# MLP products of a hybrid diffusion trunk, in seven block products in place of eight for two of three token banks

## The reference

```python
mod = silu(cond) @ mod_w[l] + mod_b[l]            # sh1, sc1, g1, sh2, sc2, g2
h = rmsnorm(x, norm_mix[l]) * (1 + sc1) + sh1
x = x + g1 * mixer(h)                              # retention or recurrence
h = rmsnorm(x, norm_mlp[l]) * (1 + sc2) + sh2
x = x + g2 * (relu(h @ mlp_w1[l]) ** 2 @ mlp_w2[l])   # 1024 -> 4096 -> 1024
```

## Time and profile before

| | us |
|---|---|
| median of 3 runs | 2734.0 (2730.71 to 2734.75) |
| the profiled execution, time | 2731.88 |
| its span | 2730.1 |
| TensorE busy | 2609.2 (96%) |
| VectorE, ScalarE, GpSimd busy | 1641.1, 666.3, 699.7 |
| DMA, mean | 66 GB/s |

### The profile page before, as it was taken

The page is one execution under the profiler, slowest core; times in us unless marked ns, Lnnn a source line. Parts: engine busy times, 40 slices in busy tenths (PEclk is TensorE's granted clock), DMA queues, the critical chain, the costliest instruction groups (busy, mean ns, idle before and its releaser), DMA issues.

```text
span 2730.1 us, 39975 instructions
## 1 busy us (share of the span) xinstructions
PE 2609.2 (96%) x14730; PEld 2524.3 (92%) x14730; DVE 1641.1 (60%) x3056; ACT 666.3 (24%) x1016; POOL 699.7 (26%) x395
## 2 busy tenths in 40 slices
PE   7999999899999999999999889789999999999998
PEld 4999999899999999999998778678999999999997
DVE  5878778548567567567586777855433443442444
ACT  5323323232001001001044544423110110110113
POOL 0221212222222222222223323432222232222321
PEclk9999999999999999999999989899999999999998
DMA  6422222312222222222222101121111111111111
GB/s 235 146 70 69 82 67 71 124 47 66 63 81 69 64 82 69 61 85 69 62 73 104 38 21 36 59 77 31 47 39 42 43 38 46 38 44 41 38 46 70
DMA packets 259139, 181.18 MB, mean 66 GB/s; under 512 B 9205, under 2 KB 253685, under 8 KB 258166
## 3 DMA queue, kind: packets, MB, share of 16 engines
q1 hardware_dynamic: 257924, 169.99, 20.4%
q10 hardware_dynamic: 1138, 10.21, 1.0%
HBM read 165.48 MB, written 14.69 MB: 66 GB/s over the span
## 4 chain that ended last, share of the span: by engine, by line
PE 85%; DVE 9%; issue 3%; ACT 2%; DMA 0%; ACTq 0%; DVEq 0%; POOL 0%; POOLq 0%; SPq 0%
PE psum L588 80%; PE psum L862 2%; DVE mod_sum L1228 2%; DVE work_f L1624 1%; DVE h_lo L1254 1%; DVE sumsq L1197 1%; PE mod_psum L613 1%; DVE x L1275 1%; PE psum L668 1%; DVE sumsq L1260 1%; DVE h_hi L1598 1%; DVE mod_sum L1223 0%; DVE s_bwd L1474 0%; PE psum L743 0%; ACT rate_f L1107 0%
## 5 line engine op out<-in xcount | busy, mean ns | idle before, releaser
L588 PE MATMUL psum<-h_hi,w_hi 128*128 128x384 f32 (+1 forms) x2880 | 682.0, 345 | 36.4 <-DVE h_lo L1254 25.6
L531 POOL CAST w_hi<-w_raw 128x1024 fp32r<-128x1024 f32 x184 | 193.5, 1052 | 1886.9 <-PE psum L588 1041.1
L588 PE MATMUL psum<-h_lo,w_hi 128*128 128x384 f32 (+1 forms) x2880 | 666.1, 340 | 0.0
L588 PE MATMUL psum<-h_hi,w_lo 128*128 128x384 f32 (+1 forms) x2880 | 663.7, 339 | 0.0
L588 PEld LDWEIGHTS psum<-h_hi,w_hi 128*128 128x128 f32 x2880 | 520.2, 191 | 48.7 <-issue 23.3
L1275 DVE SCALAR_TENSOR_TENSOR x<-psum,mod,x 128x768 f32<-128x768 f32 (+2 forms) x432 | 238.5, 610 | 476.8 <-PE psum L588 476.8
L588 PEld LDWEIGHTS psum<-h_lo,w_hi 128*128 128x128 f32 x2880 | 524.4, 190 | 0.0
L588 PEld LDWEIGHTS psum<-h_hi,w_lo 128*128 128x128 f32 x2880 | 521.3, 190 | 0.0
L533 POOL TENSOR_TENSOR w_lo<-w_raw,w_hi 128x1024 fp32r<-128x1024 f32 x184 | 445.6, 2422 | 14.7
L978 ACT ACTIVATE relu<-relu,bias 128x384 f32<-128x384 f32 x128 | 72.0, 610 | 1211.1 <-DVE relu L1326 1211.1
L588 PE MATMUL psum<-hid_hi,w_hi 128*128 128x384 f32 x1536 | 351.8, 336 | 2.8 <-DVE x L1275 2.8
(11 more groups left out here) (223 smaller groups left out, 1886.7 us busy)
## 6 DMA issues: line engine op xcount, KB each, us to landing
w_raw<-in_mlp_w SPq DMA_DIRECT2D x128, 512.0 KB, 4.0
mod_raw<-in_mod_w SPq DMA_DIRECT2D x160, 256.0 KB, 2.9
w_raw<-in_ab_w_in SPq DMA_DIRECT2D x24, 512.0 KB, 4.5
x_spill<-x ACTq DMA_DIRECT2D x2, 4608.0 KB, 13.9
w_raw<-in_lru_w_in SPq DMA_DIRECT2D x16, 512.0 KB, 4.1
x<-x_spill SPq DMA_DIRECT2D x2, 2880.0 KB, 9.6
x_rows<-in_x_sample SPq DMA_DIRECT2D x8, 512.0 KB, 7.4
scale_raw<-in_mod_w SPq DMA_DIRECT2D x8, 512.0 KB, 14.4
```

Of the source, the lines that this page charges most:

```text
L531: pool.tensor_copy(w_hi[:, s, :], w_raw[:, s, :]).then_inc(hi_done, 1)
L588: mm = pe.matmul(psum[:, s, c, 0:end - c * CH], w, v[:, k, c * CH:end], start=(first and n == 0 and w is hi[k] and v is in_hi), stop=(last ...
```

## The change

Both products of the MLP are taken in passes. A pass multiplies a 2 x 2 block of weights (four quarters A11, A12, A21, A22, each 4 tiles of 128 x 128) by a 2 x 2 block of activations. For the tokens of banks 0 and 1 (768 of 1152) the block product is made from seven products of quarters and their sums, after Winograd's form of Strassen's scheme; bank 2 keeps the four plain ones. With S1 = A21 + A22, S2 = S1 - A11, S3 = A11 - A21, S4 = A12 - S2, and on the side of the activations T1 = B12 - B11, T2 = B22 - T1, T3 = B22 - B12, T4 = B21 - T2, the products are A11 B11, A12 B21, S2 T2, S1 T1, S3 T3, A22 T4 and S4 B22. A weight sum or a B needs a split of its own into `hi` and `lo`. There are 16 passes for the first product and 16 for the second in each layer (`HALF_PASSES`, `PASSES`), each of 11 products (7 + 4) of 4 tiles by 3 matmuls. All 12 matmuls of a product go to one bank.

- **Weights.** SP loads 1 MB a pass into `wide_raw`, of which there is one, once all units of the pass before are ready (`wide_free`). GpSimd makes the four sums and all eight low parts. ScalarE makes the eight high parts, each after the step of the previous pass that last used its place.
- **First product.** VectorE joins the partial products as they are done and scales, ScalarE rectifies and squares, VectorE makes T1 to T4, and SP writes the nine entries of a pass (`stage`, 1769 KB) to a DRAM tensor `hidden`.
- **Second product.** Each pass multiplies 8 hidden tiles (4 pairs) into one pair of x tiles. Of the four pairs' entries in SBUF one is replaced in each pass: SP reads nine entries of 196 KB (`refill`), ScalarE casts, VectorE subtracts (`new_part`). Partial products are added to x in SBUF.
- **x** goes to DRAM tile by tile in `out_proj` and comes back when the second product begins.
- **h.** The first pass's entries are made from all eight tiles of `gained_out`, so TensorE's first products wait for whole entries, not for tiles.
- **Modulation of layer 1.** It is summed four columns at a time (`wide_mod`, 256 KB a load), 16 operations of 512 columns in each of passes 1 to 12 of layer 0.
- **Behind layer 0's MLP** SP loads the recurrent block's weights when VectorE has read the last bank.

The core of the diff, engine by engine.

SP:

```diff
-                u = AT_MLP[l].units
-                with sp.Fori(0, GROUPS) as g:
-                    for j in range(GRP):
-                        load_unit(g, GRP_UNITS, u + j, cols(a["mlp_w1"][l], g * (GRP * P) + j * P))
...
+                def wide_free(q):
+                    sp.wait_ge(unit_ready, q.n(STEPS, STEPS * R))
+                    sp.sem_inc(passed, 1)
...
+                def first(q, half):
+                    with_mods = l == 0 and q.j <= 2 * 6 and (q.j > 0 or q.i is not None)
+                    if with_mods:
+                        mods(q, range(2))
+                    wide_free(q.next())
+                    wide_first(q.next())
+                    if q.j or q.i is not None:
+                        store(q.last(), 1 - half)
+                    if with_mods:
+                        mods(q, range(2, KT))
...
+            sp.wait_ge(evacuated, EVACS * PASSES)
             with sp.Fori(0, KT) as b:
                 load_unit(b, BLK_UNITS, AT_MIX[1].units, cols(a["lru_w_in"][0], b * P + D_MODEL))
```

GpSimd:

```diff
+                def low(q, u, raw):
+                    pool.wait_ge(unit_cast, q.n(STEPS, STEPS * R + u + 1))
+                    pool.tensor_tensor(unit_lo[u][:], raw, unit_hi[u][:].bitcast(F32), ALU.subtract).then_inc(unit_ready, 1)
+                def units(q, first=False):
+                    S = STEPS * (R - 1)
+                    pool.wait_ge(wide_landed, q.n(32, 32 * (R + 1)))
+                    pool.tensor_tensor(unit_sum[S1][:], quarter(A21), quarter(A22), ALU.add).then_inc(unit_summed, 1)
+                    low(q, A11, quarter(A11))
...
+                    pool.tensor_tensor(unit_sum[S2][:], unit_sum[S1][:], quarter(A11), ALU.subtract).then_inc(unit_summed, 1)
+                    low(q, A21, quarter(A21))
...
+                    pool.tensor_tensor(unit_sum[S4][:], quarter(A12), unit_sum[S2][:], ALU.subtract).then_inc(unit_summed, 1)
+                    low(q, S2, unit_sum[S2][:])
+                    low(q, S1, unit_sum[S1][:])
...
+                    pool.tensor_tensor(unit_sum[S3][:], quarter(A11), quarter(A21), ALU.subtract).then_inc(unit_summed, 1)
...
+                    low(q, S3, unit_sum[S3][:])
+                    low(q, A12, quarter(A12))
+                    low(q, A22, quarter(A22))
+                    low(q, S4, unit_sum[S4][:])
```

TensorE:

```diff
+                    unit(A11)
+                    pe.wait_ge(evacuated, q.n(EVACS, V - EVACS + 4))
+                    on(B11, "a", A11).then_inc(first_done, 1)
+                    pe.wait_ge(evacuated, q.n(EVACS, V - EVACS + 5))
+                    on(PL1, "e", A11, stop=False, width=plain).then_inc(step_done, 1)
+                    unit(A21)
+                    pe.wait_ge(evacuated, q.n(EVACS, V - EVACS + 6))
+                    on(PL1, "f", A21, stop=False, width=plain).then_inc(step_done, 1)
+                    if behind:
+                        behind()
+                    unit(S2)
+                    on(T2, "b", S2).then_inc(step_done, 1)
+                    unit(S1)
+                    pe.wait_ge(evacuated, q.n(EVACS, V))
+                    on(T1, "c", S1).then_inc(step_done, 1)
+                    unit(S3)
+                    on(T3, "d", S3).then_inc(step_done, 1)
+                    unit(A12)
+                    pe.wait_ge(first_read, q.n(1, R + 1))
+                    on(B21, "a", A12)
+                    on(PL2, "e", A12, start=False, width=plain).then_inc(step_done, 1)
+                    unit(A22)
+                    on(PL2, "f", A22, start=False, width=plain)
+                    pe.wait_ge(evacuated, q.n(EVACS, V + 3))
+                    on(T4, "d", A22).then_inc(step_done, 1)
+                    unit(S4)
+                    on(B22, "c", S4).then_inc(step_done, 1)
```

ScalarE, a pass of the first product:

```diff
+                    if q.j or q.i is not None:
+                        take_first(l, q)
+                    if fills:
+                        late_part(FILL.index(PL1), PL1)
+                    unit_part(l, nq, A11)
+                    unit_part(l, nq, A21)
...
+                    unit_part(l, nq, S2)
+                    unit_part(l, nq, S1)
+                    unit_part(l, nq, S3)
...
+                    act.wait_ge(evacuated, q.n(EVACS, V + 5))
+                    act.wait_ge(scaled, q.n(4, 4 * H + 2))
...
+                    rectify(part_p, 0)
+                    rectify(out_e, 0, True)
+                    square_part(q, 1, part_p, stage[half][:, B11, :])
+                    square_part(q, 2, out_e, stage[half][:, PL1, :])
...
+                    unit_part(l, nq, A12)
...
+                    rectify(part_w, 1)
+                    rectify(out_f, 1, True)
...
+                    rectify(part_x, 1)
+                    square_part(q, 3, part_w, stage[half][:, B22, :])
+                    square_part(q, 4, out_f, stage[half][:, PL2, :])
+                    square_part(q, 5, part_x, stage[half][:, B21, :])
...
+                    unit_part(l, nq, A22)
+                    unit_part(l, nq, S4)
...
+                    rectify(part_v, 0)
+                    square_part(q, 6, part_v, part_v[:])
```

VectorE, a pass of the first product:

```diff
+                    if not opened:
+                        sums(q.last(), 1 - half)
+                        joined(q, l, 1)
...
+                    if with_mods:
+                        mods(q, range(0, 2))
+                    if not opened:
+                        joined(q, l, 2)
...
+                    dve.wait_ge(evacuated, q.n(EVACS, V + 3))
+                    scale(part_w, 1).then_inc(scaled, 1)
...
+                    if with_mods:
+                        mods(q, range(3, 6))
+                    dve.wait_ge(step_done, q.n(STEPS, S + 6))
+                    dve.tensor_tensor(part_p[:], bank("a"), part_p[:], ALU.add).then_inc(evacuated, 1)
```

848 lines of the change are left out of this document (684 added, 164 removed).

## The result

| | before | after |
|---|---|---|
| median, us | 2733.11 | 2932.84 (2930.64 to 2938.83, 4 runs) |
| ratio | | 1.0735, 95% interval 1.0716 to 1.0754 |
| the profiled execution: time, span | 2731.88, 2730.1 | 2930.64, 2928.8 |
| MLP of layer 0, of layer 1 (before: the earlier trace rows) | 836, 818 | 965, 873 |

The change makes the kernel 7.4% slower. The forecast was 2855 us, slower, with a range of 2630 to 2950. The sign, the mechanism and most of the passes came out; 78 of the 199 us that the change costs were not in the sum.

What follows compares the result with a forecast made beforehand. TensorE was taken to bound the kernel, 1654 us in the MLPs. Layer 1 + 32, layer 0 + 78 and outside edges + 11 gave + 121 on 2731.9: 2853, stated as 2855 us for the median; range 2630 to 2950.

Steps and rivals of the forecast that it cites:

- The bound now, the gain of TensorE: TensorE bounds both MLPs; 384 fewer matmuls a layer remove 134 us in all, a pass needing 22.9 us instead of 25.1.
- Cost 1, the circle: Single weight buffer: load, GpSimd, ScalarE, GpSimd, SP take 26.0 us a pass in the first product, 21.9 in the second.
- Cost 2, the turns: VectorE and GpSimd block each other in SBUF: passes become 26.6 us, 32 with modulation, 25.7 in the second product.
- Cost 3, the edges: Extra time at the MLPs' openings, between their products, behind layer 0 and at the end; edges outside the MLPs add 11 us.
- Opening and last passes: Start of an MLP: whole entries of h and roots make pass 0 34 us, pass 1 22.9, 57 together.
- The edge between the products: First to second product through DRAM: pass 16 ends 46 us after due, 23 more than its matmuls; ends 8 and 35.
- Behind layer 0: The recurrent block's first weights are asked for only when the last bank is read: 8.5 us, none before.
- The end: End of the kernel: two tiles of x are late instead of one, + 2 us.
- TensorE paces: Rival: GpSimd and VectorE rarely meet, ScalarE reaches S4 in time, a pass is 22.9 us: 2612 us; chance 0.17.
- Low ends: Rival: the circles at low terms, 1.20 us on GpSimd and 4.9 for the load: 2723 us; chance 0.20.
- Worse: Rival: GpSimd at 1.56 us adds 140 us, 2995; second clause, waiting TensorE falls to 1.2 GHz; chance 0.13.
- The signs: Trace marks: TensorE 85 to 90% busy in the MLPs, waiting on ScalarE's `part_p` and GpSimd's halves; loads 26 to 27 us apart.

Runs made afterwards that it cites:

- experiment 2: The changed kernel with ScalarE's casts of A12, A22 and S4 ahead of its rectifying and squaring in the first product: 2870.14 us, ratio 1.0498.
- experiment 1: The changed kernel with SP asking for the next weights after seven of eight unit halves, not waiting for S4's subtraction: 2883.38 us, ratio 1.0546.
- experiment 3: The changed kernel with fourteen of the sixteen modulation operations of a pass on 8 columns instead of 512, sum incomplete: 2892.37 us, ratio 1.0579.
- experiment 4: The changed kernel with SP's store of the hidden tiles issued behind the modulation's loads instead of ahead: 2913.29 us, ratio 1.0656.
- experiment 11: The changed kernel with narrow modulation operations (sum incomplete), ScalarE's casts first and the store behind the modulation's loads: 2798.89 us, ratio 1.0248.
- experiment 6: The changed kernel with VectorE's five additions of squares in the last pass put one by one between its bank reads: 2931.95 us, ratio 1.0730.
- experiment 8: The changed kernel with six edits: earlier load, casts first, store behind modulation loads, edge order, squares spread, modulation on TensorE: 2805.34 us, ratio 1.0267.
- experiment 7: The changed kernel with the modulation's products moved from VectorE's 16 operations a pass to TensorE, adding up in PSUM: 2980.87 us, ratio 1.0906.

## Why the prediction was right, and where it was short

**The sum, term by term**, by the distances of the loads, against the profiled execution:

| term | forecast | measured | missing |
|---|---|---|---|
| layer 1, 12 passes of the first product | 319.2 | 309.0 | - 10 |
| layer 1, the edge (passes 16 and 17) | 68.9 | 87.0 | + 18 |
| layer 1, 13 passes of the second product | 325.7 | 315.6 | - 10 |
| layer 1, opening and last passes | 136.2 | 161.6 | + 25 |
| layer 0, 12 intervals with modulation | 378.6 | 402.6 | + 24 |
| layer 0, two passes without | 53.2 | 50.6 | - 3 |
| layer 0, the edge | 68.9 | 85.6 | + 17 |
| layer 0, 13 passes of the second product | 325.7 | 314.3 | - 11 |
| layer 0, opening and last passes | 87.6 | 112.0 | + 24 |
| outside the MLPs | 11 | 14.2 | + 3 |

Unrounded, the missing parts add up to 77.6, which is 2930.6 - 2853. It is a sum of misses both ways: the circles were priced 34 us too high over both layers, the modulation, the edges and the ends 112 us too low.

**The bound now, the gain of TensorE.** As said. 23.3 us for a full pass (experiment 2) against 22.9. What the rival of a TensorE-paced kernel would need, ScalarE reaching S4 in time, is what experiment 2 gives it, and there it holds, in the first product alone.

**Cost 1, the circle.** Right, and three of its terms to a tenth: load 5.2 (5.2 forecast), GpSimd to S3 11.0 (11.0), SP 0.24 (0.25), with a 128x512 operation at 1.30 (1.30). ScalarE took 7.2 (7.9) and S4's subtraction 2.1 with its wait for that of A22 (1.37 + 0.3). Experiments 1 and 2 show it by moving one link each. 25.7 us against 26.6: ScalarE's 7.9 was too large, and the 0.6 for VectorE's turns lies inside GpSimd's 11.0 already (L787 1.61 above). In the second product the circle was put at 25.7 and measured 24.2: if the 21.9 without turns holds, these take 2.3 us and not 3.8.

**Cost 2, the turns.** Where both engines are at work with both their inputs in SBUF, they show in single rows. VectorE's `sums` in layer 1, one beside GpSimd's last subtraction, which began at 2291.88 and took 1.27, and the next one behind it:

```profile
2292.19 1.37 DVE L1910 TENSOR_TENSOR stage<-part_v,stage 128x384 f32<-128x384 f32 x1 [13.19 <-ACT part_v L1407]
2293.49 0.55 DVE L1911 TENSOR_TENSOR stage<-stage,part_v 128x384 f32<-128x384 f32 x1
```

The same operation takes 1.37 and 0.55 us. GpSimd's ends at 2293.15, and the long one 0.41 us later, as if it had done its work only then. The Trainium skill, *SBUF — State Buffer*, "Who interferes with whom", has the loser of the shared port blocked for the whole instruction of the other; by that rule, the trace agrees.

With the modulation the price was 32 us and the measured one 33.6, near it by luck, since it comes another way. I took GpSimd's 15.6 us as lying in VectorE's way; in the trace the circle runs through VectorE itself. ScalarE's first `rectify` waits 5.99 us for VectorE's `part_p` (L1902), and VectorE comes to it late for two reasons: it waited 5.33 us for a load of `mod_w`, which was issued behind the 1.7 MB store, and four of its operations (two take 1.41 us when GpSimd is idle) took 5.81 beside GpSimd:

```profile
937.16 2.45 DVE L1897 SCALAR_TENSOR_TENSOR wide_sum<-wide_mod,cond,wide_sum 128x512 f32<-128x512 f32 x2 [5.33 <-DMA wide_mod<-in_mod_w]
941.07 5.81 DVE L1897 SCALAR_TENSOR_TENSOR wide_sum<-wide_mod,cond,wide_sum 128x512 f32<-128x512 f32 x4
949.99 0.55 DVE L1902 TENSOR_TENSOR part_p<-part_p,sumsq 128x384 f32<-128x384 f32 x1
950.45 1.41 DVE L1897 SCALAR_TENSOR_TENSOR wide_sum<-wide_mod,cond,wide_sum 128x512 f32<-128x512 f32 x2
950.65 0.61 ACT L1403 ACTIVATE part_p<-part_p,bias 128x384 f32<-128x384 f32 x1 [5.99 <-DVE part_p L1902]
```

Experiments 3, 4 and 11 take this apart: 3.3 us go with VectorE's time, 1.8 with the store, and only all three edits come to 26.3. The step that fell short is that I named no price for SP's queue: eight loads, two at a time, with a store in front. TensorE's 16 small instructions, 1.7 us, show only once those are gone (experiment 11). I also gave the modulation 11 of the long intervals, and there are 12.

**Cost 3, the edges.** Here the forecast was short.
- *Opening and last passes*, 25 us a layer. Part of it can be read at the opening of layer 0, where TensorE waits 5.24, 2.19, 3.80 and 5.34 us between 600 and 648: for the first entry (ScalarE casts S3 and A12 ahead of PL1), for a sum's low half, for ScalarE's root, and at 647.6 for a bank read that VectorE has behind 7.37 us of reciprocals. I had counted the casts of h and not the reciprocals. At the other end the chain of experiment 6 stands. Most of the 25 us are at the opening. In layer 1 it is 84 us from its start to the fourth 1 MB load, where 57 for two passes and 3.5 to that load, which comes right behind the third pass's first product, would be 60. From the last 1 MB load to the last update it is 53.8 us in layer 0 and 50.0 in layer 1, where two passes of the forecast, less the same 3.5 us, give 48. Casts first takes 8 us off that opening of layer 1, though it was not aimed there; nothing else was tried, so the cause is read from the waits and not tested.
- *The edge between the products*, 17 us in layer 0 and 18 in layer 1. The forecast had pass 16 at 46 us, and 48 came, but it had pass 17 at 22.9, and 37.7 came. The rows: SP stores pass 15's entries at 1161.54, asks for T4 at 1168.82 once the store is out, ScalarE's cast follows at 1173.25 and VectorE's half at 1174.77. So the way of 7.3 + 4.4 us through DRAM is run twice, for PL1 and for T4. I had put this in the bounds ("only T4 late", 8 us) as an alternative, when it is an addition.
- *Behind layer 0*, 8.5 us forecast and 31.1 - 19.5 = 11.6 measured. The forecast chain is there: from VectorE's last bank read to the first weights' low half it is 1575.2 - 1565.8 = 9.4 us, and TensorE waits 14.5 for it. But the chain that ends last is another, that of experiment 6 through the eight tiles, the squares and the reciprocals, and the forecast didn't have it. It is ahead by 0.25 us only, so that the size comes out near is in part luck.
- *The end*, 2 us forecast, none measured (26.8 against 26.7 us from the last update).

**The rivals.** "TensorE paces" fell: of the stages of after, only the two passes at 1061 to 1111 us have TensorE full. "Low ends" fell with GpSimd at 1.30. "Worse" at 1.56 fell with it, but its time, 2995, was nearer than "low ends" was, and its second clause had a part: the granted clock is 0.91 to 0.97 in the stages of the first product, where TensorE waits. What the lower clock costs by itself was not separated from the waits.

**The signs.** TensorE's busy share in the MLPs is 85% and 89%, as said. The distances of the loads, 25.7, 33.6 and 24.2 us, each lie just outside what was named (26 to 27, 32, 25 to 26). The engines were not those named: TensorE's largest waits in the MLPs are for VectorE (60.6 us for `part_p` L1941, 58.9 for `x`, 57.5 for `part_x`), those for ScalarE's `part_p` come to 20.6, and none of the larger ones names GpSimd's halves.

**Why these edits do not win.** The change takes out 384 matmuls a layer, 134 us at most. From experiment 8, what it costs even with the circle open: the modulation on TensorE 12 x (30.4 - 23.3) = 85 us, the edges 2 x (79 - 47) = 64 us, together more than that. The second product, at 23.6 us where 23.3 would be matmuls alone, costs another 9.

## What to carry to other kernels

When a change takes work from the engine that paces, price the circle that the single buffer closes: load, every operation up to the last one that frees it, and on each engine whatever is queued between two of them. Then price the edges with the same care, since a pipeline that goes through DRAM, or through one buffer by turns, pays its full latency at each. A wait of the pacing engine that is removed gives time only if no chain beside it ends later; look at what follows it before it is counted.

## What the runs showed of the hardware that was not expected

- A product with two float32 operands, 128x128 by 128x2, is two instructions on TensorE, about 0.11 us apart, so 0.22 us each product (experiment 7), more than an fp32r matmul of 384 columns (0.1765). The weight load of an instruction took mostly 187 to 192 ns; whether that is what makes two columns so dear was not tested.
- A reciprocal of 384 columns takes 2.5 us on VectorE (three in 7.37), where an addition of the same size takes 0.55.
- A store of 1728 KB took 7.4 us to land, and a read of 768 KB beside others took 7.4 as well, where 192 KB took 2.4 (medians of the changed kernel).
- VectorE and GpSimd, with work queued on both, slow each other operation by operation: four modulation operations took 5.81 us beside GpSimd, where two took 1.41 without it.
